# Two-block denoiser on one core: the order in which one DMA queue carries rows and weights

## The reference, cut to what matters

```
x = x + gate * ((o * silu(gate0)) @ attn_w_out)        # "ao": attention's output projection
h = modulate(rms_norm(x))                              # transposed into hT for the next stage
...
x = x + gate * (hyena(h) @ hy_w_out); x = rms_norm(x) * final_w     # "ho"
h = modulate(rms_norm(x))
...
x = x + g1 * ([u, o] @ ev_out_w);  h = ...             # "eo"
# experts, twice (layer 0 and 1): 16 experts, two for each token
eid, gates = top2_of_best_group(sigmoid(h2 @ router_w))
for block of rows of one expert e:
    y = (silu(xb @ w1[e]) * (xb @ w3[e])) @ w2[e]
x = x + g2 * sum_of_two(gates * y)
```

## Time and profile before

| | |
|---|---|
| median of 3 runs | 4850.69 us (4841.92 to 4853.07) |
| profiled execution, its own time | 4848.21 us |
| its span | 4846.4 us |
| PE busy | 4183.6 us (86%) |
| DVE, ACT, POOL busy | 1905.8 (39%), 1095.4 (23%), 265.0 (5%) |
| mean granted TensorE clock | 0.932 of full |
| DMA | 622.86 MB, mean 129 GB/s |

### The profile page before, as it was taken

How to read it: one execution, slowest core, us unless ns; L and a number is a source line. 1 busy time by engine, 2 the same in 40 slices (tenths; PEclk the granted TensorE clock), 3 DMA queues, 4 the chain that set the end, 5 groups by cost and what they waited for, 6 DMA issues and landing times. The chain is left out here.

```text
span 4846.4 us, 59352 instructions
## 1 busy us (share of the span) xinstructions
PE 4183.6 (86%) x20951; PEld 2138.0 (44%) x20951; DVE 1905.8 (39%) x2969; ACT 1095.4 (23%) x1816; POOL 265.0 (5%) x368
## 2 busy tenths in 40 slices
PE   4899799998999998899688978867999599949995
PEld 1454455554444445777544435432333244413331
DVE  1233344443312204999646838431111333321112
ACT  0122355443111102222020236210000234100000
POOL 0100000000000000111100000000000200000001
PEclk7899899999999998999899989988999799969997
DMA  8122222114355511111430130236864511266666
GB/s 324 41 70 59 53 45 45 34 31 135 123 191 211 213 55 52 37 52 47 155 128 9 57 117 28 88 115 262 329 253 160 187 30 58 96 266 247 240 240 260
DMA packets 255634, 622.86 MB, mean 129 GB/s; under 512 B 70922, under 2 KB 149349, under 8 KB 235665
## 3 DMA queue, kind: packets, MB, share of 16 engines
q1 hardware_dynamic: 219800, 504.86, 29.5%
q0 software_dynamic: 19424, 94.01, 5.1%
q10 hardware_dynamic: 16280, 22.27, 1.3%
HBM read 1293.97 MB, written 113.53 MB: 290 GB/s over the span
## 5 line engine op out<-in xcount | busy, mean ns | idle before, releaser
L1720 PE MATMUL hyp_acc<-hy_hT,hyp_early_weights 128*128 128x512 f32 x768 | 334.8, 594 | 0.0
L3589 PE MATMUL blocks_h<-moe_w,blocks_xT 128*32 128x512 f32 x2560 | 295.6, 615 | 43.7 <-issue 43.7
L3589 PE MATMUL blocks_h<-od_hT,blocks_xT 128*32 128x512 f32 x1280 | 290.7, 608 | 26.2 <-DMA moe_w1b<-in_ex_w 21.0
L3610 PE MATMUL blocks_acc<-moe_w,blocks_hidT 128*32 128x512 f32 x2560 | 284.5, 596 | 11.3 <-DMA moe_w<-in_ex_w 10.0
L3589 PE MATMUL blocks_h<-moe_w1b,blocks_xT 128*32 128x512 f32 x1280 | 290.6, 608 | 0.0
L1045 PE MATMUL att_scores<-att_kT,att_qT 64*128 64x512 f32 (+3 forms) x768 | 251.7, 548 | 21.9 <-DMA att_v<-scratch_V 21.9
L2375 PE MATMUL evp_acc<-ev_hT,evp_early_weights 128*128 128x512 f32 x512 | 224.5, 599 | 7.6 <-DVE evp_qkT L2516 5.6
L981 DVE TENSOR_REDUCE att_nmax<-att_scores 128x1 f32<-128x1280 f32 x128 | 190.3, 1487 | 101.8 <-PE att_scores L1045 101.8
L1069 PE MATMUL att_turn<-ident,att_probs 128*128 128x128 f32 x1280 | 192.0, 280 | 42.5 <-DVE att_o L1011 22.5
L1720 PEld LDWEIGHTS hyp_acc<-hy_hT,hyp_early_weights 128*128 128x128 f32 x768 | 144.6, 191 | 173.6 <-issue 173.5
L949 ACT ACTIVATE att_probs<-att_scores,att_nmax 128x1280 f32<-128x1280 f32 x128 | 169.9, 1327 | 173.6 <-DVE att_nmax L981 171.5
(11 more groups left out here) (542 smaller groups left out, 6390.1 us busy)
## 6 DMA issues: line engine op xcount, KB each, us to landing
moe_w<-in_ex_w SPq DMA_DIRECT2D x320, 2048.0 KB
od_hT<-in_ex_w SPq DMA_DIRECT2D x80, 2048.0 KB
moe_w1b<-in_ex_w SPq DMA_DIRECT2D x80, 2048.0 KB
hyp_m_weights<-in_mod_w POOLq DMA_DIRECT2D x6, 8192.0 KB, 24.3
mod_weights<-in_ada_w SPq DMA_DIRECT2D x12, 2048.0 KB, 20.6
scratch_y_rows<-blocks_x ACTq DMA_DIRECT2D x40, 512.0 KB, 9.2
hyp_early_weights<-in_hy_w_in SPq DMA_DIRECT2D x8, 2048.0 KB
scratch_parts<-hyp_uT SPq DMA_DIRECT2D x24, 512.0 KB, 3.7
```

The lines of the kernel that those rows point to most:

```text
L1720: mm = nc.tensor.matmul(acc[:, m % 2, half * NC:(half + 1) * NC], weights[:, ws, kt, c:c + P], hT[:, kt, half * NC:(half + 1) * NC], start ...
L3589: mm = nc.tensor.matmul(out[mine, :], xT[:, kt, mine], w[l][:, kt, :], start=(kt == 0), stop=(kt == KT - 1))
L3610: mm = nc.tensor.matmul(acc[mine, c, :], hidT[:, kt, mine], w2[l][:, kt, c * NC:(c + 1) * NC], start=(kt == 0), stop=(kt == FT - 1))
```

## The change

In `project_out` both first row tiles are issued ahead of the stage's own weights, the loop is written out, both row loads of a pair are issued ahead of the residual loads and stores of it, and the next stage's weights are handed out one piece for each turn of that loop, behind the pair's row loads, where all were issued ahead of the loop before. In `moe_blocks` the wait for the landed gathers in front of w3 is gone; in front of w2 there is a wait for `asked`.

```diff
 # project_out, SP
-                for c in range(2):
-                    load_a(0, c)
-                    if early is None:
+                for s in range(S):
+                    load_a(0, s)
+                if early is None:
+                    for c in range(2):
                         load_out_weights(sp, w, weights, w_in, c)
                 for s in range(S):
                     load_x(0, s)
@@
-                if ahead is not None:
-                    ahead[0](sp)
-                with sp.Fori(0, TT // S - 1) as i:
+                for i in range(TT // S - 1):
                     for s in range(S):
                         load_a(i + 1, s)
+                    if ahead is not None:
+                        ahead[0](sp, i)
+                    for s in range(S):
                         load_x(i + 1, s)
                         store(i, s)
                         store_h(i, s)
 # hyena_weights
-    def load(sp):
+    def load(sp, i):
+        if i == TT // 2 - 2:
+            return
+        if i == 0:
+            load_taps(sp)
         wv = d["hy_w_in"][0].rearrange("(kt p) n -> p kt n", p=P)
-        for s in range(2):
-            sp.dma_start(weights[:, s, :, :], wv[:, :, s * NC:(s + 1) * NC]).then_inc(w_in[s], 16)
+        sp.dma_start(weights[:, i, :, :], wv[:, :, i * NC:(i + 1) * NC]).then_inc(w_in[i], 16)
 # even_weights
-    def load(sp):
-        sp.dma_start(tap_rows[:, :], d["ev_dw_w_2"][0]).then_inc(taps_in, 16)
+    def load(sp, i):
+        if i == 0:
+            sp.dma_start(tap_rows[:, :], d["ev_dw_w_2"][0]).then_inc(taps_in, 16)
         wv = d["ev_in_w_2"][0].rearrange("(kt p) n -> p kt n", p=P)
-        for c in (1, 0, 2):
-            sp.dma_start(weights[:, c, :, :], wv[:, :, c * NC:(c + 1) * NC]).then_inc(w_in[c], 16)
+        c = (1, 0, 2)[i]
+        sp.dma_start(weights[:, c, :, :], wv[:, :, c * NC:(c + 1) * NC]).then_inc(w_in[c], 16)
 # moe_blocks, SP
                 for m, dst in enumerate((w1, w3, w2)):
-                    if m == 1:
-                        for s in range(S):
-                            sp.wait_ge(x_in[s], 16)
+                    if m == 2:
+                        sp.wait_ge(asked, signals(S))
                     for l in range(LANES):
                         load_part(sp, d, layer, dst[l], m, each[l]).then_inc(w_in[l][m], 16)
```

More of the change, by code:

```diff
@@ L1778, in hyena_weights, with load_taps @@
     w_in, taps_in = [sem(f"w_in{s}") for s in range(2)], sem("taps_in")
-    def load(sp):
+    def load_taps(sp):
         sp.dma_start(tap_rows[0:TAPS * rows, :], d["hy_conv_w"][0].rearrange("j (q p) -> (j q) p", p=P)).then_inc(taps_in, 16)
         sp.dma_start(tap_rows[TAPS * rows:, :], d["hy_conv_b"].rearrange("a (q p) -> (a q) p", p=P)).then_inc(taps_in, 16)
+    def load(sp, i):
[3 more added lines that the diff above has]
+            load_taps(sp)
         wv = d["hy_w_in"][0].rearrange("(kt p) n -> p kt n", p=P)
-        for s in range(2):
-            sp.dma_start(weights[:, s, :, :], wv[:, :, s * NC:(s + 1) * NC]).then_inc(w_in[s], 16)
+        sp.dma_start(weights[:, i, :, :], wv[:, :, i * NC:(i + 1) * NC]).then_inc(w_in[i], 16)
     return (weights, w_in, tap_rows, taps_in), (load, w_in + [taps_in])
```

## The result

The changed kernel takes 4815.12 us (median of 4 runs, 4815.02 to 4817.37) against 4851.88 (4841.92 to 4853.22) for the kernel before in the same comparison: ratio 0.9936, 95% interval 0.9923 to 0.9948. A second comparison gave 4817.75 against 4844.9, ratio 0.9948 (0.9935 to 0.9961). The forecast was 4821, in a range of 4810 to 4834. The profiled execution's span is 4813.4 us, against 4846.4.

What follows compares the result with a forecast made beforehand. PE, busy 86% of the span, was taken as the bound, so only its idle time behind transfers could pay. ho 18.8, ao 1.3, eo 0 and experts 6.8 sum to 26.9 us: 4848.2 becomes 4821, range 4810 to 4834.

Steps and rivals of the forecast that it cites:

- ho, order of landing: In ho, third tile's rows become ninth MB, not fifteenth, at 2.93 us each; with the clock, 18.8 us gained (17.3 to 19.3).
- Rival C: In ho, row loads move at half the weights' rate, so rows land 8.8 us later: 4830 us; chance 0.06.
- What meets at the third tile: In ho, third tile's rows and PE's free time meet; transposes start at 2418.8 against 2436.25: 17.4 us.
- The clock: In ho, the pause before the first 32 matmuls costs 1.4 to 2.2 us; third tile's work runs 1.4 us shorter.
- Rival B: In ho, all first 32 matmuls run at 1.2 GHz, 27.8 us, losing 11.7 of the gain: 4833 us; chance 0.06.
- Pieces hidden: In ho and ao loops, weight pieces stay hidden; if not, each costs at most 5.9 us for ho's three.
- ao: In ao, third tile starts right as the 32 matmuls end: 1.3 us gained (1.1 to 1.4).
- Loop, eo: Loop written out in three stages: 0, between 0.5 lost and 0.3 won each; eo's earlier row loads: 0.
- Experts: In both experts' stages w3 lands 3.4 us earlier, PE's 12.95 us wait shrinks to some 9.5: 6.8 us together.
- Rival A: Experts gain nothing, as the queue loses as much elsewhere: 4828 us; chance 0.11.
- rival E: Start of experts' stages: gathers starve until weights are through, +25 us in experts 0, about +9 in experts 1: 4862; chance 0.03.
- Rival D: Experts' 19 further steps also gain 3 us a stage and ho sits at its upper bound: 4814 us; chance 0.07.

Runs made afterwards that it cites:

- kernel 2: The kernel before with only the experts' edit (w3 right behind w1, w2 after `asked`), projections as before: 4840.71 us against 4847.27, ratio 0.9990.
- kernel 1: The kernel before with only the output projections' edits, the experts' list as before: 4823.1 us against 4847.27, ratio 0.9951.
- Kernel 5: The changed kernel, but w2 waits for both landed gathers instead of `asked`: 4817.01 us beside the changed kernel's 4817.75.
- kernel 6: The changed kernel, in ho half 0 of its own weights in two pieces and rows(1,0) ahead of x and constant rows: 4815.97 us against 4817.75.
- 9: The changed kernel with each piece of next-stage weights between slot 0's and slot 1's row loads: 4816.35 us against 4843.11 for the kernel before.
- kernels 3: The kernel before with only both first row tiles issued ahead of the stage's own weights: ratio 0.9993 to the kernel before.
- kernel 8: The kernel before with only the projections' row loop written out, no load moved: 4845.71 us against 4843.11, ratio 1.0005.
- kernel 7: The changed kernel with each piece of next-stage weights issued ahead of the pair's row loads: 4838.85 us, ratio 0.9990 to the kernel before.

## Why the prediction came out right, step by step

The predicted sum was 26.9 us. The four stretches, each averaged over the profiles that have the edit and those that don't (for ho and ao: before twice and kernel 2, against the changed kernel twice, kernels 1 and 5), give ho 170.2 - 152.5 = 17.7, ao 145.2 - 143.9 = 1.3, the first steps 50.05 - 46.6 = 3.4 and 49.55 - 45.8 = 3.7 (old and new heads): 26.1 us. The ratios of the five kernels that have both parts whole or nearly (changed twice, 5, 6, 9) average 0.9944, or 27 us. The first comparison's 31 was at the favourable end of that: in its profile PE's busy time was the lowest of all thirteen, which is sooner luck than the change.

- *ho, order of landing.* Right in kind: fifteenth MB to ninth. The 32 matmuls began 9.79 us behind the first gate, 2.1 earlier than the 11.92 of before; 3.05 were forecast. **This term was mis-sized**: one price, 2.93 us, for every MB. The second tile's rows took 3.19 us and the first half of weights about 3.3 a MB (2400.21 - 2393.61 = 6.6 for 2 MB), while the eight MB up to the third tile's rows took 22.92, 2.87 each. Rival C, rows at half the rate of weights, is out: the third gate came 22.92 us behind the first and not some 9 later. The end of ho's gain is 17.7 in place of 18.8, inside the bounds.
- *What meets at the third tile.* The forecast had the rows land as PE came free; they were there 1.6 us ahead. So PE's own work is now the bound, and the start of the first matmuls decides, which is what kernel 6 used.
- *The clock.* The pause ahead of the first matmuls was to cost 1.4 to 2.2 us. In the first profile it cost 2.2 (16.14 - 13.90, the granted clock 0.54, nearly all at 1.2 GHz, up to 2405 and 1.00, 2.4 GHz, from there). In the second profile of the changed kernel, line below, and in kernel 1 the same matmuls took 17.03 and 17.02 us, 3.1 over 13.90. That is beyond the forecast and past the 17 us that the prediction had named as a sign of being wrong: **a second term that was mis-sized**, and the reason why ho is 152.9 and 153.0 us there and not 152.1. The total held because 0.9 us are little in its range. Rival B, all 32 matmuls at 1.2 GHz, is out. That the third tile's clock loss vanishes with its pause held; kernels 3 and 8 show that the loss may be 2.1 us and not 0.5, so in such an execution of the kernel before the gain is larger.

```profile
2399.38 17.03 PE L1509 MATMUL ho_acc<-ho_weights,ho_aT 128*128 128x512 f32 x32 [3.60 <-DMA ho_weights<-in_hy_w_out]
```

- *Pieces hidden.* Right in the changed kernel (PE's wait for hyp's first weights is 3.2 us, 3.3 before, and evp has none), under a condition that the forecast had only half: hidden behind slot 0's rows, not behind rows at large, and worth far more than the 5.9 us apiece of the queue's time if they aren't: 6.6 us each in kernel 7, since a late gate holds the normalisation behind it and PE then works at the lower clock.
- *ao.* 1.0 by the first profile, 1.3 over several; the first 32 matmuls took 15.73 in place of 15.31, the clock again.
- *Loop, eo.* The loop is nothing by kernel 8's whole time. In eo, from the first row's issue to the last matmul of the folded rows, the profile has 148.1 us before (3084.6 to 3232.7) and 148.4 after (3060.0 to 3208.4), and PE's wait for the first rows is 9.8 (9.9 in the earlier trace rows): nothing, as forecast.
- *Experts.* 3.4 and 3.7 against 3.4 each, and PE's wait 9.50 where some 9.5 was said. Rival A is out. The gather came through beside the weights: PE waited 12.95 us for x(0), 12.47 before, and not 39 more, which ends rival E. From its issue to PE's first use x(0) took 11.5 us, 11.05 before (second profiles: 12.2 and 11.0), within the 1 or 2 us allowed. The forecast's rival E put the point where the gain is used up at x(0) landing at 3305; that counts the loss in full in both stages. With the 15.63 us that it lets experts 1 absorb, the same figures give some 3312. Kernel 5 shows that the new wait costs nothing and that w2's earlier issue brings nothing.
- *Rival D* claimed the same place as the first comparison (4814), with later steps gaining 3 us a stage. The averages above speak against it, and ho is under the forecast, not at its upper bound.

What stays open: *other* averages 3640.8 us over the five profiles without the pieces and 3638.9 over the eight with the pieces; with single values from 3636.3 to 3642.2 in the latter these 1.9 us are not shown to be the change's.

## What to carry to other kernels

In a queue that lands in order, count for each load the MB ahead of it, and put weights for later behind the rows whose consumer stands next in line. Which rows are urgent is read from the consumer's own in-order list: here the rows of one slot of two, because their gate stands ahead of work that the bottleneck engine waits for. A bulk load that holds back nothing urgent is free; the same load one place further ahead cost 6.6 us a piece and the whole gain of the stage.

## What the runs showed of the hardware

- A gather moves beside a full queue of weights. In the changed kernel q0 took a fifth of the DMA engines' time from 3250 to 3262 while the total stayed at 426 GB/s, so the weights lose what the gather takes:

```profile
DMA packets 543, 5.11 MB, mean 426 GB/s; under 512 B 47, under 2 KB 47, under 8 KB 292
...
q1 hardware_dynamic: 281, 4.10, 79.8%
q0 software_dynamic: 261, 1.00, 20.4%
```

  That is 1.00 MB in 12 us, 83 GB/s, above the 65 taken as the lower bound from the earlier trace rows.
- The length of the same work behind a pause is not fixed. After 14.3 to 16.5 us of idle time on PE and the same eight transposes, the third tile's 32 matmuls in ho took 14.40, 14.47, 15.29, 15.96 and 15.97 us (the kernel before twice, kernels 2, 8 and 3), against 13.90 at the full clock; the first tile's took 16.14 and 17.03 in two executions of the changed kernel. A stretch measured across such a pause is uncertain by 1.6 us.
